# Gated delta rule in nine steps a tile instead of ten, with its norms in the next tile and part of the output projection beside its last steps

## The chip, the cores and the metric

One NeuronCore of one Trainium2 chip runs the whole program. The metric is the device time of one execution in microseconds (us); lower is better. The kernel before took 2258.96 us, the median of three runs (2255.09 to 2261.31).

## What is computed

Three residual blocks over 512 tokens of width 1024: two layers (mLSTM with forgetting attention; SSD with pooling), each with a convolved FFN, and then a third block, whose mixer is a gated delta rule (GDN) gated together with a sparse attention. The change touches only the GDN and the projection behind it. Cut to that:

```python
G = jnp.cumsum(gc, axis=-1)
gamma = jnp.exp(jnp.where(tri, G[..., :, None] - G[..., None, :], -jnp.inf))
A = jnp.where(strict, jnp.einsum("bnhid,bnhjd->bnhij", kb, kc) * gamma, 0.0)
T = lax.linalg.triangular_solve(A + eye, eye, left_side=True, lower=True)
v_new = u_i - jnp.einsum("bhcd,bhde->bhce", w_i, state)
o = jnp.einsum("bhcd,bhde->bhce", qg_i, state) + jnp.einsum("bhij,bhje->bhie", att_i, v_new)
state = state * dl_i[..., None, None] + jnp.einsum("bhcd,bhce->bhde", kd_i, v_new)
o_gdn = rmsnorm(o_gdn, gdn_norm_g[l]) * jax.nn.silu(z)
mixed = sigmoid(gate_a + gb[:D]) * o_gdn + sigmoid(gate_b + gb[D:]) * o_dsa
h = h + jnp.einsum("bse,ed->bsd", mixed, w_out[l])
```

## The kernel before

The weights are a stream of 333 units of 128x1024 fp32 that SP's queue loads into a ring of six slots. ACT rounds each unit to a high part (`whi`, L1015) and DVE subtracts it to get the low part (`wlo`, L1636); a product of two matrices is three matmuls, high by high, high by low, low by high (L370, L371, L372). A unit's slot is free when `units_done` counts it.

The GDN works on 4 tiles of 128 tokens and 8 heads. The heads are two groups `g` of four; group 0 owns PSUM banks 0 to 3, group 1 banks 4 to 7. A tile of a group goes through parts 0 to 9, written in each engine's program under `for c, g, part in gdn_order` (PE L909, ACT L1505, POOL L1596, DVE L2283). `gdn_order` sets every engine's order by hand: group 0 takes one part, then group 1 takes the part that lies five behind, and so on through 45 slots. The names in the code are these:

- part 0: `gb`, `bb`, `ge` (bf16 matmuls that spread gates and decays), `kq` (keys by queries); ACT makes `gam` and `eg`, DVE the gated keys `kb` (L2291), POOL copies the inverted 32x32 diagonal blocks into place (`placed`, L1605 and L1608);
- part 1: `kk`, then transposes `kt` and `vt` (L932, L938); DVE `at` (L2295) and `att` (L2298), POOL `kbg` and the squared queries `qq` (L1616);
- part 2: `x5`; DVE `kd` (L2301). Part 3: `y5`. Part 4: `x6`; DVE `qg` (L2314). Part 5: `y6`. These four products of 4 heads by 64 columns build the inverse of the 128x128 triangle from the small blocks, each waiting for a copy of the one before by ACT or DVE;
- part 6: `ks`, keys by state; DVE `r` (L2318). Part 7: `vn`, the new values; ACT copies them;
- part 8: `o`, the output (L984, L986), and `s`, the state's increment; ACT squares `o`, DVE adds the squared queries (L2322), gates `o` (`og`, L2323) and updates the state (L2328);
- part 9: `ms`, the mean of squares by a matmul with 1/128 (L997); ACT takes Ln and Exp (L1538, L1540), DVE scales (`scaled`, L2334), POOL adds into `MIX` (`mixed`, L1620).

The diagonal blocks are inverted before, by `substitute` on DVE (L2221, L2223), spread over the units of the projection `gatea` by the table `solved`, with two transposes after the last row (L2272, L2273).

After the last part ACT rounds `MIX` tile by tile (`split_tile`, L1038), DVE makes the low parts (L2343), and PE starts the projection `out2` with units 0 to 3 and tiles 0 to 2 (`token_products`, L444).

## Time and profile before

| | us |
|---|---|
| median of three runs | 2258.96 |
| the profiled execution | 2262.21 |
| its span | 2260.4 |
| busy: PE | 2196.7 |
| busy: DVE | 1297.4 |
| busy: ACT | 918.5 |
| busy: POOL | 110.7 |

The profile is of one execution. Busy time of PE is the time in which a matmul is in the array, counted to its modelled end, so back-to-back matmuls overlap: the distance from one start to the next is what a matmul costs. PEld is the load of its stationary operand. PEclk is the granted clock, 1.00 at 2.4 GHz and 0.50 at 1.2 GHz. "<-" names what ended an idle time. The GDN lies from 1711 us to 1834 us of the span.

### The profile page before, as it was taken

The page shows a single profiled execution, that of the slowest core. Times are in us where ns is not written, and L with a number is a line of the kernel's source. Part 1 is how long each engine was busy: PE and PEld are TensorE (multiplying, and loading weights), DVE is VectorE, ACT ScalarE, POOL GpSimd, SP SyncE. Part 2 cuts the span into 40 slices and gives each one's busy share as a digit, 9 for nine tenths or more (in the row PEclk, how much of TensorE's full clock was granted, in tenths as well). Part 3 has the DMA queues.
Part 4 walks back from the last instruction along what each step waited for, and adds up shares of the span by engine and source line. Part 5 has one row for each costly group of instructions (what it writes and reads, how often), then busy time and mean ns, then how long its engine had stood idle before and what let it go on. Part 6 is the DMA issues. An engine that isn't in the chain of part 4 may idle for free.

```text
span 2260.4 us, 26898 instructions
## 1 busy us (share of the span) xinstructions
PE 2196.7 (97%) x10736; PEld 1797.9 (80%) x10744; DVE 1297.4 (57%) x1995; ACT 918.5 (41%) x1544; POOL 110.7 (5%) x133
## 2 busy tenths in 40 slices
PE   8999999999999999999999999999998989999998
PEld 7867788888888668888888887776887868888887
DVE  6355475555347667555535439646786636555534
ACT  4135553334344545333434434344444434333431
POOL 1000040000000003000000000000002410000000
PEclk9999999999999999999999999999998999999999
DMA  5212223333323113333332222112221002333332
GB/s 198 89 56 75 66 85 94 102 94 111 103 71 105 58 45 105 94 101 95 111 104 77 88 88 75 47 44 78 84 85 38 1 32 81 95 101 94 117 98 75
DMA packets 50668, 189.82 MB, mean 84 GB/s; under 512 B 5617, under 2 KB 5617, under 8 KB 49777
## 3 DMA queue, kind: packets, MB, share of 16 engines
q1 hardware_dynamic: 50544, 188.11, 26.6%
q8 instruction: 86, 1.41, 0.3%
q14 instruction: 38, 0.30, 0.0%
HBM read 185.99 MB, written 2.10 MB: 83 GB/s over the span
## 4 chain that ended last, share of the span: by engine, by line
PE 89%; DVE 6%; ACT 2%; issue 2%; DMA 1%; ACTq 0%; DVEq 0%
PE bank L370 26%; PE bank L371 25%; PE bank L372 25%; PE bank L863 3%; PE bank L646 1%; PE bank L624 1%; PE bank L482 1%; PE bank L635 1%; PE bank L837 1%; DMA ring<-stream 1%; ACT whi L1015 1%; PE bank L562 1%; DVE small L1662 1%; DVE wlo L1636 0%; DVE small L1796 0%
## 5 line engine op out<-in xcount | busy, mean ns | idle before, releaser
L370 PE MATMUL bank<-xs,whi 128*128 128x512 f32 (+2 forms) x1992 | 772.8, 388 | 9.6 <-DVE xs L1984 7.8
L372 PE MATMUL bank<-xs,wlo 128*128 128x512 f32 (+2 forms) x1992 | 751.9, 377 | 0.0
L371 PE MATMUL bank<-xs,whi 128*128 128x512 f32 (+2 forms) x1992 | 751.4, 377 | 0.0
L1636 DVE TENSOR_TENSOR wlo<-ring,whi 128x1024 fp32r<-128x1024 f32 x333 | 415.1, 1249 | 317.4 <-ACT whi L1015 317.2
L1015 ACT ACTIVATE whi<-ring 128x1024 fp32r<-128x1024 f32 x333 | 350.1, 1053 | 283.1 <-DMA ring<-stream 280.8
L370 PEld LDWEIGHTS bank<-xs,whi 128*128 128x128 f32 x1992 | 376.9, 189 | 89.5 <-issue 7.9
L372 PEld LDWEIGHTS bank<-xs,wlo 128*128 128x128 f32 x1992 | 376.3, 189 | 69.5
L371 PEld LDWEIGHTS bank<-xs,whi 128*128 128x128 f32 x1992 | 377.2, 189 | 68.0 <-issue 3.3
L370 PE MATMUL bank<-whi,xs 128*128 128x512 f32 (+1 forms) x816 | 321.0, 393 | 9.8 <-DVE wlo L1636 5.7
L371 PE MATMUL bank<-wlo,xs 128*128 128x512 f32 (+1 forms) x816 | 317.9, 390 | 0.0
L372 PE MATMUL bank<-whi,xs 128*128 128x512 f32 (+1 forms) x816 | 317.5, 389 | 0.0
L1300 ACT ACTIVATE arena<-bank,par 128x512 f32<-128x512 f32 x132 | 103.0, 780 | 433.2 <-PE bank L372 433.2
L1927 DVE SCALAR_TENSOR_TENSOR arena<-bank,par,arena 128x511 f32<-128x511 f32 x132 | 98.9, 749 | 286.9 <-ACT arena L1300 286.7
L370 PEld LDWEIGHTS bank<-whi,xs 128*128 128x128 f32 x816 | 155.6, 191 | 43.0 <-DVE wlo L1636 7.5
L372 PEld LDWEIGHTS bank<-whi,xs 128*128 128x128 f32 x816 | 155.6, 191 | 31.9
L371 PEld LDWEIGHTS bank<-wlo,xs 128*128 128x128 f32 x816 | 155.8, 191 | 30.6 <-issue 0.2
L1929 DVE SCALAR_TENSOR_TENSOR arena<-bank,par,arena 128x510 f32<-128x510 f32 x132 | 98.8, 749 | 4.7
L1779 DVE SCALAR_TENSOR_TENSOR arena<-bank,par,arena 128x511 f32<-128x511 f32 (+2 forms) x96 | 71.8, 748 | 46.7 <-ACT arena L1461 36.2
L1571 POOL TENSOR_TENSOR arena<-arena 128x512 f32<-128x512 f32 x32 | 52.6, 1683 | 499.6 <-PE bank L482 307.1
L1152 ACT ACTIVATE arena<-bank,small 128x128 f32<-128x128 f32 (+3 forms) x64 | 33.7, 527 | 72.6 <-DVE small L1796 72.3
L1796 DVE TENSOR_REDUCE small<-bank 128x1 f32<-128x128 f32 (+3 forms) x64 | 31.2, 488 | 50.2 <-PE bank L626 46.8
L1461 ACT ACTIVATE arena<-bank,par 128x512 f32<-128x512 f32 x24 | 16.5, 687 | 87.6 <-PE bank L372 87.6
(319 smaller groups left out, 1927.9 us busy)
## 6 DMA issues: line engine op xcount, KB each, us to landing
ring<-stream SPq DMA_DIRECT2D x333, 512.0 KB, 3.6
arena<-gains SPq DMA_DIRECT2D x5, 1024.0 KB, 5.7
arena<-xt SPq DMA_DIRECT2D x4, 512.0 KB, 6.3
arena<-xn SPq DMA_DIRECT2D x1, 2048.0 KB, 7.9
out<-arena SPq DMA_DIRECT2D x4, 512.0 KB, 2.6
con<-consts SPq DMA_DIRECT2D x1, 744.0 KB, 11.6
arena<-brow SPq DMA_DIRECT2D x1, 512.0 KB, 12.3
par<-params SPq DMA_DIRECT2D x1, 407.5 KB, 8.0
```

The lines of the kernel that those rows point to most:

```text
L370: nc.tensor.matmul(out, ah, bh, start=first, stop=False)
L371: nc.tensor.matmul(out, ah, bl, start=False, stop=False)
L372: return nc.tensor.matmul(out, al, bh, start=False, stop=last)
L863: m = nc.tensor.matmul(tile(b)[:, hh, 0:n], l(hh), r(hh), start=start, stop=stop)
L1015: A(whi[:, v % SLOTS, :], ring[:, v % SLOTS, :], ACT.Copy).then_inc(whi_done, 1)
L1152: A(st["ps"][:, 0:W], bank[2 + n % 3][:, 0:W], ACT.Exp, bias=small[:, 200 + n % 4:201 + n % 4], accum_out=small[:, 204 + n % 4:205 + n % 4 ...
L1300: A(acc[:, s, :], bank_of(up, j)[:], ACT.Identity, bias=col(cols, 4 * j + 3), scale=col(cols, 4 * j + 2)).then_inc(scalar_out, scalar_at.n ...
L1571: nc.gpsimd.tensor_tensor(XT[:, tt, h], XT[:, tt, h], GB[:, i, h], op).then_inc(gpsimd_out, gpsimd_at.next("gained" if i == 0 else "shifte ...
L1636: V.tensor_tensor(wlo[:, v % SLOTS, :], ring[:, v % SLOTS, :], whi[:, v % SLOTS, :], ALU.subtract).then_inc(wlo_done, 1)
L1779: STT(dst[:, shift:], u[:, 0:SEQ - shift], w, dst[:, shift:], ALU.mult, ALU.add).then_inc(vector_out, vector_at.next())
L1927: STT(acc[:, s, 1:], u[:, 0:SEQ - 1], col(cols, 4 * j + 1), acc[:, s, 1:], ALU.mult, ALU.add).then_inc(vector_out, vector_at.next())
L1929: STT(acc[:, s, 2:], u[:, 0:SEQ - 2], col(cols, 4 * j), acc[:, s, 2:], ALU.mult, ALU.add).then_inc(vector_out, vector_at.next("conv", l, j))
```

## The change

- `LAG` is 4 and `STEPS` 9: group 1 lies four parts behind group 0, and part 9 is gone.
- The norm of a tile is done in the same group's next tile: sums of squares and `ms` in part 0, Ln and Exp in part 3, `scaled` in part 4, `mixed` on POOL in part 5. For that the outputs are kept in the place of the tile's queries (`outputs`), squares and roots in `kd`. The squared queries are made by ACT in part 6, no longer by POOL.
- `kq` moves from part 0 to part 3 and `att` to part 4; `kt` from part 1 to part 5 and `kd` to part 6, and both are left out in the last tile, which needs neither.
- The stationary operands of `x5` and `y5` have 96 columns, those of `x6` and `y6` 64, and the copies read the rows that are left.
- The splits of units 3, 4 and 5 of `out2`, three in a row in tile 1 before, are put into part 6 of three steps. The row table `solved` ends one unit of `gatea` earlier.
- In the last tile of group 1 the sixteen high-part products of tile 0 of `out2` (units 0 to 3) stand in parts 6 and 7; the eight low-part ones and the last `ms` follow the last part. `split_tile(0)` and `(1)` on ACT and the low part of tile 0 on DVE move up beside them.

```diff
-        HALF_STEP, STEPS = 5, 10
+        LAG, STEPS = 4, 9
+        out2_splits = {(0, 1): FIRST["out2"] + 3, (1, 0): FIRST["out2"] + 4, (1, 1): FIRST["out2"] + 5}
         gdn_order = []
-        for n in range(STEPS * TILES + HALF_STEP):
+        for n in range(STEPS * TILES + LAG):
             if n < STEPS * TILES:
                 gdn_order.append((n // STEPS, 0, n % STEPS))
-            if n >= HALF_STEP:
-                gdn_order.append(((n - HALF_STEP) // STEPS, 1, (n - HALF_STEP) % STEPS))
+            if n >= LAG:
+                gdn_order.append(((n - LAG) // STEPS, 1, (n - LAG) % STEPS))
...
+                    if (j, tt, half) in begun:
+                        done[j, tt, half] = nc.tensor.matmul(bank[b][:], xlo[:, slot(j), t], whi[:, s, w], start=False, stop=j == n - 1)
+                    else:
+                        done[j, tt, half] = products(bank[b][:], (xhi[:, slot(j), t], xlo[:, slot(j), t]), (whi[:, s, w], wlo[:, s, w]), j == 0, j == n - 1)
...
+                def high(j, tt, half):
...
+                    begun.add((j, tt, half))
+                    nc.tensor.matmul(bank[b][:], xhi[:, slot(j), t], whi[:, s, w], start=j == 0, stop=False)
+                    nc.tensor.matmul(bank[b][:], xhi[:, slot(j), t], wlo[:, s, w], start=False, stop=False)
...
                     if part == 0:
...
-                        claim(b + 3)
-                        pe.wait_ge(scalar_out, scalar_at.find("gqkv", 15))
-                        four(b + 3, lambda hh: gk[:, 4 * g + hh, cs], lambda hh: gq[:, 4 * g + hh, cs]).then_inc(tensor_out, tensor_at.next("kq", t))
...
+                        if c:
+                            mean_square(c - 1, g)
...
-                        four(b + 3, lambda hh: G["at"][:, hh, :], lambda hh: G["t5"][:, hh, :], n=64).then_inc(tensor_out, tensor_at.next("x5", t))
...
+                        four(b + 1, lambda hh: G["at"][:, hh, BLOCK:], lambda hh: G["t5"][:, hh, :], 3 * BLOCK, 64).then_inc(tensor_out, tensor_at.next("x5", t))
...
+                        four(b, lambda hh: G["at"][:, hh, 64:P], lambda hh: G["t6"][:, hh, :], 64, 64).then_inc(tensor_out, tensor_at.next("x6", t))
...
                     elif part == 6:
...
+                        if t == (TILES - 1, 1):
+                            mean_square(TILES - 1, 0)
+                            pe.wait_ge(scalar_out, scalar_at.find("xh", "mix2", 0))
+                            for j in (0, 1):
+                                for half in (0, 1):
+                                    out2_part.high(j, 0, half)
...
+                        reader[b + 1] = (SCALAR, ("sq", t)) if c < TILES - 1 else (VECTOR, ("og", t))
...
+                for j in range(4):
+                    for half in (0, 1):
+                        out2_part(j, 0, half)
+                mean_square(TILES - 1, 1)
...
+                    elif part == 3 and c:
+                        inverse_root(c - 1, g)
...
+                    elif part == 6:
+                        if t == (TILES - 1, 1):
...
+                        A(query_squares(c, g), outputs(c, g), ACT.Square).then_inc(scalar_out, scalar_at.next("qq", t))
+                        if t in out2_splits:
+                            split_units(out2_splits[t])
...
-                    nc.gpsimd.tensor_tensor(G["qq"], gq[:, 4 * g:4 * g + 4, cs], gq[:, 4 * g:4 * g + 4, cs], ALU.mult).then_inc(gpsimd_out, gpsimd_at.next("qq", t))
...
+                elif part == 5 and c:
+                    done = slice((c - 1) * P, c * P)
+                    pool.wait_ge(gpsimd_out, gpsimd_at.n)
+                    pool.wait_ge(vector_out, vector_at.find("scaled", (c - 1, g)))
+                    nc.gpsimd.tensor_tensor(MIX[:, 4 * g:4 * g + 4, done], MIX[:, 4 * g:4 * g + 4, done], outputs(c - 1, g), ALU.add).then_inc(gpsimd_out, gpsimd_at.next("mixed", (c - 1, g)))
...
-                solved = (8, 11, 14, 17, 20, 23, 26, 29, 31)
+                solved = (8, 12, 16, 19, 22, 25, 28, 31, 31)
...
                     if part == 0:
+                        if c:
+                            square_sums(c - 1, g)
                         dve.wait_ge(tensor_out, tensor_at.find("bb", t))
-                        if c:
-                            dve.wait_ge(vector_out, vector_at.find("scaled", (c - 1, g)))
                         V.tensor_tensor(G["kb"], gk[:, 4 * g:4 * g + 4, cs], tile(b + 1), ALU.mult).then_inc(vector_out, vector_at.next("kb", t))
...
                     elif part == 4:
+                        dve.wait_ge(tensor_out, tensor_at.find("kq", t))
+                        dve.wait_ge(vector_out, vector_at.find("at", t))
+                        V.tensor_tensor(G["gam"], tile(b + 2), G["gam"], ALU.mult).then_inc(vector_out, vector_at.next("att", t))
+                        if c:
+                            scaled(c - 1, g)
+                    elif part == 5:
+                        if t == (TILES - 1, 1):
+                            square_sums(TILES - 1, 0)
...
+                    elif part == 7:
+                        if t == (TILES - 1, 1):
+                            scaled(TILES - 1, 0)
+                            mixed(TILES - 1, 0)
                     elif part == 8:
-                        dve.wait_ge(scalar_out, scalar_at.find("sq", t))
-                        dve.wait_ge(gpsimd_out, gpsimd_at.find("qq", t))
-                        STT(G["gam"], G["qq"], RMS_EPS * P * P, G["gam"], ALU.mult, ALU.add).then_inc(vector_out, vector_at.next("sq", t))
-                        STT(gated, tile(b + 1), small[:, 224:225], z2[:, 4 * g:4 * g + 4, cs], ALU.mult, ALU.mult).then_inc(vector_out, vector_at.next("og", t))
+                        if t == (TILES - 1, 1):
+                            dve.wait_ge(tensor_out, tensor_at.find("vn", t))
+                            tile_low(0)
+                        dve.wait_ge(tensor_out, tensor_at.find("o", t))
+                        dve.wait_ge(scalar_out, scalar_at.find("qq", t) if c < TILES - 1 else scalar_at.find("sq", t))
+                        dve.wait_ge(vector_out, vector_at.find("qg", t))
+                        STT(outputs(c, g), tile(b + 1), small[:, 224:225], z2[:, 4 * g:4 * g + 4, cs], ALU.mult, ALU.mult).then_inc(vector_out, vector_at.next("og", t))
...
+                square_sums(TILES - 1, 1)
+                tile_low(1)
+                tile_low(2)
+                scaled(TILES - 1, 1)
+                mixed(TILES - 1, 1)
+                tile_low(3)
```

How the orders move, at three places. In the names, bank0 to bank3 are group 0 and bank4 to bank7 group 1.

PE, around the end of part 8 of group 0 in a middle tile. Before (L863 is `s`, then `y5` of group 1, L997 `ms`, L863 `x6`, then part 0 of group 1):

```order
L863 MATMUL bank6<-arena,scratch 128x128 x4
L863 MATMUL bank0<-scratch 128x64 x4
L997 MATMUL bank7<-arena,inv128 128x512
L863 MATMUL bank2<-scratch 128x64 x4
L868 MATMUL bank4<-arena 128x128
...
L863 MATMUL bank5<-arena 128x128 x4
```

and now (L892 `s`, `x6` of group 1, the gates of group 0's next tile, L942 its `ms`, L892 `y6`, L1001 `kt`):

```order
L892 MATMUL bank2<-arena,scratch 128x128 x4
L892 MATMUL bank4<-scratch 64x64 x4
L897 MATMUL bank0<-arena 128x128
L898 MATMUL bank0<-mtb,idb 128x128
...
L892 MATMUL bank1<-arena 128x128 x4
L892 MATMUL bank2<-arena 128x128 x4
L942 MATMUL bank3<-scratch,inv128 128x512
L892 MATMUL bank5<-scratch 64x64 x4
L1001 MATMUL bank6<-con,arena 128x128 x4
```

`ms` of a tile now stands behind the gates of the next tile, and `y6`, `kt` and the next `kk` stand behind it.

DVE, behind part 8 of one group. Before (sums of squares L2322, `og` L2323, the state L2328, `decays` and `qg` of the other group L2310 and L2314, `scaled` L2334, the next `kb` L2291):

```order
L2322 SCALAR_TENSOR_TENSOR arena<-scratch,arena 128x512
L2323 SCALAR_TENSOR_TENSOR scratch<-bank,small,arena 128x512
L2328 SCALAR_TENSOR_TENSOR arena<-arena,small,bank 128x128 x4
L2310 COPY small<-arena 128x4
L2314 TENSOR_TENSOR arena<-arena 128x512
L2334 TENSOR_TENSOR scratch<-scratch,arena 128x512
L2291 TENSOR_TENSOR arena<-arena,bank 128x512
L2318 TENSOR_TENSOR scratch<-scratch,bank 128x512
```

and now (`og` L2430, the state L2435, `att` and `scaled` of the other group L2395 and L2360, the sums of squares L2354, the next `kb` L2381):

```order
L2430 SCALAR_TENSOR_TENSOR arena<-bank,small,arena 128x4x128
L2435 SCALAR_TENSOR_TENSOR arena<-arena,small,bank 128x128 x4
L2395 TENSOR_TENSOR arena<-bank,arena 128x512
L2360 TENSOR_TENSOR arena<-arena,scratch 128x4x128
L2354 SCALAR_TENSOR_TENSOR scratch<-scratch 128x512
L2381 TENSOR_TENSOR arena<-arena,bank 128x512
L2402 COPY small<-arena 128x4
L2406 TENSOR_TENSOR arena<-arena 128x512
L2385 SCALAR_TENSOR_TENSOR scratch<-bank,arena 128x512
```

The sums of squares, for which `ms` waits, left the place ahead of `og` and stand behind the state and two operations of the other group.

PE at the end. Before (L863 is `x6`, `y6`, `ks`, `vn` of group 1, L984 and L986 `o`, L997 `ms`, then `out2`):

```order
L863 MATMUL bank7<-arena,scratch 128x128 x4
L863 MATMUL bank4<-scratch 128x128 x4
L984 MATMUL bank5<-arena 128x128
L986 MATMUL bank5<-arena 128x128
...
L997 MATMUL bank7<-arena,inv128 128x512
L370 MATMUL bank0<-whi,xs 128x512
L371 MATMUL bank0<-wlo,xs 128x512
L372 MATMUL bank0<-whi,xs 128x512
```

and now (L892 is `x6`, `y6`, `ks`, L942 the `ms` of group 0, L467 and L468 high-part products, L892 `vn`, L1036 and L1038 `o`, L453 low-part products):

```order
L892 MATMUL bank4<-scratch 64x64 x4
L892 MATMUL bank5<-scratch 64x64 x4
L892 MATMUL bank7<-arena,scratch 128x128 x4
L942 MATMUL bank3<-arena,inv128 128x512
L467 MATMUL bank0<-whi,xs 128x512
L468 MATMUL bank0<-wlo,xs 128x512
...
L892 MATMUL bank4<-scratch 128x128 x4
L467 MATMUL bank0<-whi,xs 128x512
...
L1036 MATMUL bank5<-arena 128x128
L1038 MATMUL bank5<-arena 128x128
...
L453 MATMUL bank1<-whi,xs 128x512
...
L942 MATMUL bank7<-arena,inv128 128x512
L383 MATMUL bank2<-whi,xs 128x512
```

Twenty-four products of `out2` that stood behind the last `ms` now lie around `vn` and `o`.

## Rows read from the trace of the kernel before

**Rows 1.** The page: busy time and share of each engine over the span.

```profile
PE 2196.7 (97%) x10736; PEld 1797.9 (80%) x10744; DVE 1297.4 (57%) x1995; ACT 918.5 (41%) x1544; POOL 110.7 (5%) x133
```

**Rows 2.** Windows: stretch, its length, busy time (instructions) per engine, PEclk, DMA.

```profile
1711.13:1739.04 27.91, 23.07 (x164) 21.23 (x164) 14.15 (x26) 12.77 (x32) 9.69 (x22) 0.82 0.06 20
1739.04:1769.59 30.55, 25.93 (x215) 24.03 (x215) 20.19 (x37) 15.74 (x37) 12.00 (x22) 0.94 0.00 1
1769.59:1796.71 27.12, 25.89 (x230) 24.27 (x230) 17.34 (x35) 12.79 (x34) 11.99 (x22) 1.00 0.01 2
1796.71:1817.40 20.69, 20.33 (x188) 19.51 (x188) 13.71 (x25) 10.33 (x29) 10.70 (x21) 1.00 0.00 1
1817.40:1845.51 28.11, 19.33 (x103) 15.49 (x102) 12.39 (x18) 10.98 (x17) 1.29 (x2) 0.88 0.00 1
```

**Rows 3.** Timeline of PE, second to third tile: start, us, line, operation, count.

```profile
1759.32 1.06 PE L863 MATMUL bank<-arena 128*128 128x128 f32 x8
1760.21 0.60 PE L932 MATMUL bank<-con,arena 128*128 128x128 f32 x4
...
1763.16 0.44 PE L984 MATMUL bank<-arena 128*128 128x128 f32 x2
...
1765.00 1.06 PE L863 MATMUL bank<-arena,scratch 128*128 128x128 f32 x8
1765.90 1.00 PE L863 MATMUL bank<-scratch 128*128 128x64 f32 x8
1766.74 1.08 PE L997 MATMUL bank<-arena,inv 128*128 128x512 f32 x2
...
1771.45 1.00 PE L863 MATMUL bank<-scratch 128*128 128x64 f32 x8
```

**Rows 4.** Groups by form: weight loads of 128 and of 8 columns.

```profile
L863 PEld LDWEIGHTS bank<-scratch 128*128 128x128 f32 x320 | 40.6, 199 | 13.2 <-DVE scratch L2305 6.0 <-ACT scratch L1524 2.9 <-DVE arena L2298 2.0
...
L601 PEld LDWEIGHTS bank<-arena,con 128*8 128x8 f32 x16 | 0.8, 87 | 2.8 <-issue 2.8
```

**Rows 5.** Timeline of DVE, third tile.

```profile
1770.13 1.71 DVE L2314 TENSOR_TENSOR arena<-arena 128x512 f32<-128x512 f32 x1
...
1782.41 1.11 DVE L2328 SCALAR_TENSOR_TENSOR arena<-arena,small,bank 128x128 f32<-128x128 f32 x4
...
1783.71 0.69 DVE L2314 TENSOR_TENSOR arena<-arena 128x512 f32<-128x512 f32 x1
```

**Rows 6.** Timeline of POOL, same stretch.

```profile
1770.02 1.26 POOL L1620 TENSOR_TENSOR arena<-arena,scratch 128x512 f32<-128x512 f32 x1 [5.57 <-DVE small L2310]
```

**Rows 7.** Timeline of DVE, end of the projection before the delta rule.

```profile
1709.74 0.21 DVE L2221 TENSOR_TENSOR arena<-arena 128x60 f32<-128x60 f32 x1
...
1710.69 2.02 DVE L2272 STREAM_TRANSPOSE arena<-arena 128x1024 f32<-128x1024 f32 x1
```

**Rows 8.** Timeline of all engines, last steps of the last tile.

```profile
1824.81 1.11 PE L863 MATMUL bank<-arena,scratch 128*128 128x128 f32 x8
...
1825.96 0.69 DVE L2318 TENSOR_TENSOR scratch<-scratch,bank 128x512 f32<-128x512 f32 x1 [0.23 <-PE bank L863]
...
1826.79 1.13 PE L863 MATMUL bank<-scratch 128*128 128x128 f32 x8 [0.87 <-DVE scratch L2318]
```

**Rows 9.** Timeline of PE, start of the output projection.

```profile
1837.35 0.77 PE L370 MATMUL bank<-whi,xs 128*128 128x512 f32 x1 [4.07 <-issue]
...
1845.51 0.39 PE L370 MATMUL bank<-whi,xs 128*128 128x512 f32 x1
```

**Rows 10.** Windows of a few microseconds, for PEclk.

```profile
1716.00:1720.00 4.00, 4.00 (x22) 3.73 (x22) 1.98 (x3) 1.88 (x7) 3.45 (x10) 0.58 0.00 0
1724.00:1730.00 6.00, 5.49 (x34) 5.47 (x34) 0.90 (x2) 2.38 (x7) 0.00 (x0) 0.50 0.01 3
1750.50:1754.00 3.50, 3.50 (x18) 3.50 (x18) 2.81 (x6) 0.60 (x1) 0.00 (x0) 0.53 0.00 0
1828.00:1836.00 8.00, 3.12 (x18) 2.16 (x18) 2.63 (x4) 4.75 (x7) 0.00 (x0) 1.00 0.00 0
```

190 lines of the change are left out of this document (110 added, 80 removed).

## Prediction

> **What bounds the kernel now.** PE is busy for 97% of the span [rows 1], so elsewhere only PE's own work counts. I read the delta rule apart, by windows from one `gb` of group 0 to the next: the first two tiles take 27.9 and 30.6 us, a settled one 27.1, the last one 20.7 to group 0's `o`, and from there it is 28.1 to the point at which 24 of `out2`'s products are issued [rows 2]. Together 134.4 us, the only stretch that the change touches. In the settled tile PE is the limit: it is busy for 25.9 of the 27.1 [rows 2] and its starts follow each other [rows 3]. In the two first tiles and at the end it waits for the other engines, and the clock falls with it [rows 2, 10].
>
> **PE's work in half a tile.** From start to start, four fp32 products of 128 columns cost 0.90 us, eight (`o`) 1.84, four of 64 columns 0.84 [rows 3]. The time shown for a group is 0.16 longer than that, for its modelled end; so four transposes are 0.44 and `ms` 0.91. From `gb` at 1769.59 to `y6` at 1771.45 lie the bf16 gates and `kq` [rows 2, 3]: 1.86, less 0.90, leaves 0.95 for the gates. Before, each group's tile holds `o`, five of 0.90, two sets of transposes, four of 0.84, `ms` and the gates: 12.4 us, so 24.9 for both groups, and 27.1 with waits.
>
> **The narrower operands.** The 64-column products cost as much as a load of 128 columns, 0.105 us each, half of what their moving side alone would need being below it (128 columns take 0.11). A load took 199 ns for 128 columns and 87 ns for 8 [rows 4], so about 0.9 ns a column. With 96 columns each of the eight takes 0.08 and the four 0.64; with 64, 0.053 and 0.43. That is 2 x 0.20 + 2 x 0.41 = 1.2 us less per half tile (one group's tile): 11.2. The bounds are 0 (a load is no shorter for fewer columns) and 1.2; I take 1.2, since the two rows differ so widely.
>
> **What takes the place of it.** The new order puts `ms` of a tile behind a queue on DVE. From the issue of the last `s` product: 0.25 to its result, the state 1.14, `att` 0.61, `scaled` 0.61, the sums of squares 0.69, 0.14 to PE: 3.4 us (durations [rows 5, 8], each 0.08 less where the next one follows, whose start overlaps; the lags, 0.04 to DVE and 0.14 to PE, [rows 8]). Meanwhile PE has only `x6` 0.43 and the gates 0.95, so it waits 2.0 us, and `y6`, `kt` and the next `kk` stand behind `ms`. Two smaller waits, for `x5`'s copies and for `r`, add 0.8. Half a tile is then 11.2 + 2.8 = 14.0, a tile 27.8: in a settled tile the change gives back more than the narrower operands win.
>
> **The walk.** To get the four stretches I walked every engine's queue through both orders, each instruction at the later of its engine's free time and its releaser's end plus the lag, with the durations above. Of the order before it gives 30.5, 26.8 and 20.5 us for tile 1, tile 2 and the way from the last `gb` to the last `o` of group 0, where the trace has 30.6, 27.1 and 20.7. Of the new order:
> - Tile 0: 19.0 at full clock. The trace has 27.9 where the walk has 23.8 at full clock and 28.2 with the clock halved in the first two stretches of [rows 10]. The rows of `substitute` that no longer stand in the last unit of `gatea` are 0.95 us of DVE [rows 7] on the way to the first `kb`. The first wait of PE stays over 2 us, so the clock falls once or twice again: 20.3 or 22.5. I take 22.0, 5.9 less than before.
> - Tile 1: 27.2, 3.4 less. The three splits in a row, behind which PE waited, are spread.
> - Tile 2: 27.8, 0.7 more.
> - The end: 39.8, 9.0 less. Up to `o` of group 0 it is 23.6 against 20.7, two more waits for `ms`. From there, before, 28.1 us: six waits of PE, 8.8 in all, 0.87 ahead of `vn` [rows 8] and 4.07 ahead of the first product; and 24 products in 8.2 us, where at 0.23 each (0.39 less 0.16) they take 5.5: 2.7 for the clock [rows 9]. Now PE has `o` 1.8, `x6` and `y6` 0.9, `ks` 0.9, `ms` 0.9, high parts 1.8, `vn` 0.9, high parts 1.8, `o` 1.8, low parts 1.8, `ms` 0.9: 13.5, and waits 0.8 for `x6`'s copy, 1.0 for the sums of squares and 0.8 at the last `ms`: 16.1. No wait is long, so I leave the clock at full. The tile's own transposes `kt`, left out here, are 0.9 of it.
>
> Sum: 22.0 + 27.2 + 27.8 + 39.8 = 116.8 against 134.4. I take 17 of the 17.6, since the walk of the order before came out 0.6 short over 78 us. The profiled execution took 2262.2, so 2245.2; it stood 3.3 above the median of 2258.96, so the median becomes **2242.0**.
>
> **Taken at nothing.** ACT gets the squared queries, 0.6 us twice a tile, from POOL: it is busy 12.8 of 27.1 us [rows 2] and they lie behind `ks`, where it has nothing to do. If that cover were gone, `vn`'s copy would be late by 0.6. POOL loses 1.04 us per half tile. No DMA moves: the ring's slots are freed by `units_done` as before, and SP's queue issues the same loads. The first six `gatea` units carry up to one more row pair of `substitute` on DVE, whose splits are three units ahead.
>
> **A rule against a row.** `qg` on DVE took 1.71 us while POOL's L1620 ran from 0.11 us before it, and 0.69 alone [rows 5, 6]: it waited until POOL was done. In the walk such waits cost 0.9 us in all. The Trainium skill ("SBUF — State Buffer", "Who interferes with whom") says more: a DVE instruction with two SBUF inputs and a GpSimd instruction that reads SBUF exclude each other for a whole instruction, whoever comes first. By it `scaled` and the sums are stopped as well where they meet POOL. POOL is busy for 12.0 of 27.1 us with 22 instructions [rows 2], 0.55 us each; three such instructions in each of eight half tiles, met 44 times in 100 and halfway, would wait 24 x 0.44 x 0.27 = 2.9 us, 2 more than in the sum; that is inside the range.
>
> **The rivals.**
> 1. *The clock falls in each half tile.* PE's wait for `ms` is 1.7 to 2.0 us, with small gates beside it. Behind longer waits of PE in the first two tiles the clock was at half for 3.5 to 6 us; against it, from 1828 to 1836 PE was busy 3.1 of 8 us and the clock stayed 1.00 [rows 10]. If each of the six middle waits is followed by 3.4 us at half, the walk gives 126.2 for the 116.8: 8.2 gained, **2251**. The Trainium skill ("TensorE: Matmul & The Clock Gate", "What's actually happening") calls the throttled clock the default that only activity releases, which speaks for this one. Chance 0.15.
> 2. *Narrow operands load no faster.* The walk is then 5.1 longer: 2242 + 5 = **2247**. Against it, the 87 ns row. Chance 0.07.
> 3. *The clock stays down through the delta rule.* Half a tile is then 11.2 x 2 + 2 = 24.4 instead of 14, six times: 62 more, **2304**. It decides from about 34 us at 1.2 GHz, where 17 us of PE's work doubled eat the gain. Before, it was down for some 20 us of 134, and PE's share of work now falls from 92% to 80% of the time. Chance 0.04.
> 4. *The high parts do not fill.* They stand in PE's queue ahead of `vn` and wait for ACT's rounding of tile 0, which waits for POOL's last sums. In the walk it is 1.2 us early; late by 3, the end is 3 longer: **2245**. Chance 0.06.
>
> **How the numbers follow.** The forecast has 0.68, its own range 2236 to 2249: tile 0 between 20.3 and 24, and 3 us either way for the medians, whose runs spread over 6. Rivals 1, 2 and 4 are faster too, 1 hardly. Range for 8 in 10: 2235 to 2253. A difference under 0.3%, 6.8 us, is not told from none: faster means below 2252.2. That is 0.68 + 0.08 + 0.06 + 0.04 = 0.86; same 0.09, slower 0.05.
>
> **What would show it.** The profile after should show, counted from the first `gb`: the second some 22 us later, then 27 and 28; PE's `ms` preceded by an idle time of 1.5 to 2 us put down to DVE's sums of squares; the four products of 64 columns start to start in 0.43 and those of 96 in 0.64; PEclk 1.00 from tile 1 to the end; and no gap over 1.1 us between group 0's last `o` and the first product of tile 1 of `out2`, 16 us apart. I am wrong if a settled tile is under 26 or over 29 us, or if the end is not 8 us shorter.

## The result and the profile after

| | before | after |
|---|---|---|
| median, us | 2259.75 | 2243.45 |
| lowest to highest | 2255.09 to 2261.31 | 2242.39 to 2246.15 |
| profiled execution | 2262.21 | 2243.9 |
| its span | 2260.4 | 2242.1 |

Four runs of each; the ratio is 0.9929, 95% interval 0.9916 to 0.9943, 16 us less. Forecast were 2242.0 and faster. The page:

```profile
PE 2180.8 (97%) x10728; PEld 1779.5 (79%) x10736; DVE 1300.5 (58%) x1993; ACT 923.6 (41%) x1552; POOL 106.2 (5%) x125
```

The stretches between the `gb` of group 0, then to its last `o` and to the first product of tile 1 of `out2` (windows, columns as in [rows 2]):

```profile
1708.95:1731.45 22.50, 18.39 (x157) 16.41 (x156) 10.90 (x21) 11.81 (x31) 9.64 (x28) 0.85 0.09 24
1731.45:1758.65 27.20, 23.07 (x214) 20.11 (x213) 18.07 (x34) 15.87 (x39) 10.87 (x19) 1.00 0.01 2
1758.65:1788.68 30.03, 26.14 (x230) 23.10 (x228) 20.15 (x36) 14.92 (x38) 11.01 (x20) 0.94 0.01 1
1788.68:1812.70 24.02, 20.62 (x194) 18.27 (x193) 16.82 (x31) 13.08 (x36) 7.98 (x12) 1.00 0.00 1
1812.70:1828.81 16.11, 14.63 (x95) 11.60 (x93) 10.28 (x15) 7.68 (x12) 1.58 (x1) 1.00 0.00 1
```

119.86 us where [rows 2] have 134.38, 14.5 less. The two spans differ by 18.3. The rest lies outside: the first `gb` stands at 1708.95 instead of 1711.13, and from the last point to the end it is 413.3 us instead of 414.9. Whether the 2.2 us ahead of the stretch are scatter is not settled. In the twelve other profiles of this study, whose code up to there is nearly the same, the first `gb` lies between 1705.96 and 1711.19. But the two profiles of the order before have the two latest, 1711.13 and 1711.19, and they alone show the clock at 0.50 for 3.4 us at 1440 us; the twelve of the changed order end at 1710.44. The 1.6 us behind it are about one more stretch at half clock, which the profile before has at 1867 us.

A settled half tile (PE's timeline, from one `gb` at 1788.68 to the next at 1802.58; the gates' bf16 products stand between the first two rows):

```profile
1788.07 0.68 PE L892 MATMUL bank<-scratch 128*64 128x64 f32 x8
...
1789.16 0.61 PE L892 MATMUL bank<-arena 72*128 72x128 bf16 x8
1791.25 1.10 PE L942 MATMUL bank<-scratch,inv 128*128 128x512 f32 x2 [1.48 <-DVE scratch L2354]
1792.28 0.68 PE L892 MATMUL bank<-scratch 128*64 128x64 f32 x8
1792.88 0.66 PE L1001 MATMUL bank<-con,arena 128*128 128x128 f32 x4
...
1796.63 1.78 PE L892 MATMUL bank<-scratch 128*128 128x128 f32 x16 [0.22 <-ACT scratch L1595]
```

The reader is to see one wait, 1.48 us ahead of `ms` (L942), put down to DVE's sums of squares (L2354), and one of 0.22 ahead of `vn`. The row names ACT's squares (L1595) for the second; by the program PE waits there for `r`, which DVE ended 0.14 us earlier, and never for the squares. And from start to start: `y6`, four products with 64 columns loaded, take 0.60 (1792.28 to 1792.88), not 0.43. DVE in the same moments:

```profile
1788.18 1.12 DVE L2435 SCALAR_TENSOR_TENSOR arena<-arena,small,bank 128x128 f32<-128x128 f32 x4
1789.22 0.68 DVE L2395 TENSOR_TENSOR arena<-bank,arena 128x512 f32<-128x512 f32 x1
1789.82 0.68 DVE L2360 TENSOR_TENSOR arena<-arena,scratch 128x512 f32<-128x512 f32 x1
1790.42 0.68 DVE L2354 SCALAR_TENSOR_TENSOR scratch<-scratch 128x512 f32<-128x512 f32 x1
1791.02 0.68 DVE L2381 TENSOR_TENSOR arena<-arena,bank 128x512 f32<-128x512 f32 x1
...
1792.36 1.76 DVE L2406 TENSOR_TENSOR arena<-arena 128x512 f32<-128x512 f32 x1
```

State, `att`, `scaled`, sums of squares, `kb`: PE's `ms` stands behind the fourth. The weight loads (groups by form, tiles 1 to 3; beside [rows 4]):

```profile
L892 PEld LDWEIGHTS bank<-arena,scratch 128*128 128x128 f32 x80 | 9.7, 192 | 0.0
L892 PEld LDWEIGHTS bank<-scratch 128*96 128x96 f32 x88 | 8.5, 165 | 2.6 <-ACT scratch L1577 2.6
...
L892 PEld LDWEIGHTS bank<-scratch 128*64 128x64 f32 x80 | 5.8, 146 | 4.7 <-issue 4.1
```

Half tile 20 to 21 (`gb` of group 0 of tile 2 to that of group 1) took 16.14 us instead of 13.9. The clock fell behind its wait for `ms`:

```profile
1762.00:1764.00 2.00, 2.00 (x11) 1.33 (x11) 1.90 (x2) 0.30 (x1) 1.47 (x2) 0.50 0.00 0
1764.00:1766.00 2.00, 2.00 (x15) 2.00 (x14) 0.11 (x2) 0.08 (x1) 0.00 (x0) 0.68 0.00 0
```

The clock is 1.6 of the 2.2 us, and 0.7 is a split. From `ms` to `y5` it is 8.54 us here and 6.99 in the half tile before it, which has the same split and full clock. In both, ACT's split of a unit stands ahead of `x5`'s copies, and PE waits for them (ACT, PE); in the settled half tile above, without a split, it does not:

```profile
1767.95 1.07 ACT L1066 ACTIVATE whi<-ring 128x1024 fp32r<-128x1024 f32 x1
```

```profile
1769.76 0.86 PE L892 MATMUL bank<-scratch 128*96 128x64 f32 x8 [0.48 <-ACT scratch L1577]
```

And the end, where [rows 8] and [rows 9] show waits of 0.87 and 4.07 us (PE; `y6`, `ms` of group 0, `ms` of group 1, tile 1 of `out2`; the high and low parts of tile 0 stand between the two `ms`):

```profile
1815.79 0.65 PE L892 MATMUL bank<-scratch 128*64 128x64 f32 x8 [0.53 <-ACT scratch L1582]
...
1818.08 1.10 PE L942 MATMUL bank<-arena,inv 128*128 128x512 f32 x2 [0.55 <-DVE arena L2354]
...
1827.76 1.10 PE L942 MATMUL bank<-arena,inv 128*128 128x512 f32 x2 [0.40 <-DVE arena L2354]
1828.81 0.50 PE L383 MATMUL bank<-whi,xs 128*128 128x512 f32 x1
```

No wait over 0.55 is left, and from `o` at 1812.70 to 1828.81 it is 16.1.

### The profile page after: what moved, and what is told of

It reads as the page before. It is cut to its first block, busy times and chain, and to the rows that moved or that the text cites. A ratio compares the mean times of both kernels' runs of the same rounds, so it can differ in the third digit from the quotient of the medians.

```text
span 2242.1 us, 26904 instructions
## 1 busy us (share of the span) xinstructions
PE 2180.8 (97%) x10728; PEld 1779.5 (79%) x10736; DVE 1300.5 (58%) x1993; ACT 923.6 (41%) x1552; POOL 106.2 (5%) x125
## 4 chain that ended last, share of the span: by engine, by line
PE 88%; DVE 7%; ACT 3%; issue 2%; DMA 1%; POOL 0%; DVEq 0%; ACTq 0%; POOLq 0%
PE bank L383 26%; PE bank L385 25%; PE bank L384 25%; PE bank L892 2%; PE bank L675 1%; PE bank L653 1%; DMA ring<-stream 1%; ACT whi L1066 1%; PE bank L511 1%; DVE small L1729 1%; PE bank L664 1%; PE bank L866 1%; PE bank L591 1%; DVE arena L1756 1%; DVE wlo L1703 0%
## 5 line engine op out<-in xcount | busy, mean ns | idle before, releaser
L383 PE MATMUL bank<-whi,xs 128*128 128x512 f32 (+1 forms) x808 | 315.5, 391 | 5.6 <-DVE wlo L1703 5.6
L384 PE MATMUL bank<-wlo,xs 128*128 128x512 f32 (+1 forms) x808 | 312.6, 387 | 0.0
L385 PE MATMUL bank<-whi,xs 128*128 128x512 f32 (+1 forms) x808 | 312.5, 387 | 0.0
L383 PEld LDWEIGHTS bank<-whi,xs 128*128 128x128 f32 x808 | 152.8, 189 | 37.8 <-DVE wlo L1703 7.4
L385 PEld LDWEIGHTS bank<-whi,xs 128*128 128x128 f32 x808 | 152.8, 189 | 31.0
```

The lines of the kernel that those rows point to most:

```text
L383: nc.tensor.matmul(out, ah, bh, start=first, stop=False)
L384: nc.tensor.matmul(out, ah, bl, start=False, stop=False)
L385: return nc.tensor.matmul(out, al, bh, start=False, stop=last)
```

## Experiments

All are edits of the changed kernel but for one of the kernel before. They were measured in four groups on different chips, each beside the kernel before, whose medians were 2258.5 to 2259.6 us; medians of different groups compare to about 1 us. Half tiles are read from `gb` to `gb`; "a drop" is a stretch in which one-microsecond windows show the granted clock at 0.50.

### The changed kernel again

This run is called the repeat below.

> The changed kernel once more, word for word, beside the runs of one change to it each. Theory of a noisy clock: half tile 20 to 21 took 16.1 us in the first profile because the granted clock was 0.69 from 1760 to 1765; in this profile the half tiles from the second gb of tile 1 on are all 13.9 (within 0.2), and the drop stands elsewhere or is not there, so that the stretch from the first gb to the first product of tile 1 of out2 is 117.5 rather than 119.9 us. Rival, a drop that the program causes: the same half tile is 16 us again. The part ahead of the first gb, whose code is the same but for the rows of substitute, ended 2.2 us earlier than before: if that is scatter between executions, this profile puts it anywhere between 1708.5 and 1711.5. Time against the kernel before: 0.993, as in the first measurement.

Measured: 2244.2 us (2242.92 to 2246.06, 5 runs), ratio to before 0.9939 (0.9927 to 0.9950). Windows of its profile, tile 2 and the end, from the last `gb` of group 0 to the first product of tile 1:

```profile
1757.41:1787.46 30.05, 26.17 (x231) 22.74 (x229) 20.16 (x36) 14.92 (x38) 11.02 (x20) 0.94 0.01 1
1787.46:1829.15 41.69, 36.81 (x287) 31.09 (x285) 27.15 (x45) 20.74 (x47) 9.56 (x13) 0.96 0.00 1
```

The half tile 20 to 21 is 16.14 again, to the hundredth: the rival holds there, the drop comes from the program. But a second drop, at 1804, was not in the first profile and costs 1.6 (26.23 from the last `gb` to tile 1 became 27.79), and tile 0, with the clock at half for 3.4 us instead of 6.8, was 1.1 shorter (21.39). Where a drop falls is partly the program's, partly not. The first `gb` came at 1708.82 once more.

### 128 columns loaded again

```
-four(b + 1, lambda hh: G["at"][:, hh, BLOCK:], lambda hh: G["t5"][:, hh, :], 3 * BLOCK, 64)
+four(b + 1, lambda hh: G["at"][:, hh, :], lambda hh: G["t5"][:, hh, :], P, 64)
...
```

The same for `y5`, `x6`, `y6`; the copies read the rows where the results then stand.

> The changed kernel with the four small product groups (x5, y5, x6, y6) loading 128 columns again, and nothing else changed. Theory (a load costs its columns, 0.9 ns each, and the loads set the pace of a 64-column product): each group is 0.84 us from start to start instead of 0.64 and 0.43, a half tile 1.2 longer in PE's work; the walk through the queues gives 5.1 us more than the changed kernel (some of it falls into waits): 2248.5 against 2243.4, the settled tile 29.0 instead of 27.8. Rival, the products are paced by something other than the number of columns loaded: 0 us, and 0.84 in both. Second rival, PE's work does not matter since DVE's queue ahead of ms sets the half tile: under 1.5 us, with the idle time ahead of ms shorter by what the products are longer.

Measured: 2248.4 us, 12 runs from 2241.5 to 2258.0, far more scattered than the others; ratio to before 0.9960 (0.9946 to 0.9974). The profiled run was the slowest:

```profile
1710.44:1739.89 29.45, 25.83 (x157) 24.54 (x157) 11.06 (x22) 12.07 (x31) 9.64 (x28) 0.65 0.05 19
1739.89:1767.69 27.80, 24.33 (x215) 22.44 (x214) 18.11 (x35) 15.85 (x39) 10.54 (x19) 1.00 0.01 1
1767.69:1798.41 30.72, 27.48 (x231) 25.30 (x231) 20.18 (x36) 14.90 (x38) 10.99 (x20) 0.94 0.01 1
1798.41:1840.63 42.22, 38.50 (x287) 33.61 (x286) 27.04 (x44) 20.59 (x47) 9.55 (x13) 0.96 0.00 1
```

In its tile 0 the clock stood at 0.50 for 20 us, from 1716 to 1736, though PE had work for 25.8 of 29.5 us. Where the clock is full, the half tiles are 13.15, 14.65 and 14.18 us where the changed kernel has 12.85, 14.35 and 13.90: 0.3 longer each, not 0.6 as in the walk; the wait ahead of `ms` shrank from 1.48 to 1.35. So the second rival is right about the settled tiles: the work saved falls mostly into waits for DVE. The windows at full clock give 2 to 2.5 us in all; the median's 4.2 are nearer to the walk's 5.1, but where the rest lies no run shows. The scatter goes with the clock: the mean granted clock of the twelve runs goes from 0.995 (2241.5 us) to 0.986 (2258.0 us), four of them at 0.988 or less, and the two fastest are under every run of the changed kernel. At 0.992 and 0.993 the wide runs took 2246.1 to 2247.2 us, the changed kernel's 2242.4 to 2246.2.

### The narrow operands alone, in the kernel before

```
-four(b, lambda hh: G["at"][:, hh, :], lambda hh: G["t6"][:, hh, :], n=64)
+four(b, lambda hh: G["at"][:, hh, 64:P], lambda hh: G["t6"][:, hh, :], rows=64, n=64)
...
```

> The kernel before with the narrower operands alone: x5, y5, x6 and y6 load 96, 96, 64 and 64 columns and write as many rows, ten steps a tile and all else as before. Theory: the walk through the order before gives 2.4 us less, 2257.3 for 2259.7 (of 1.2 us a half tile, 9.6 in all, three quarters fall into waits of PE behind DVE and ACT). Rival, PE's work is the whole limit in this stretch: 8 to 10 us less, 2250.5. Rival, the load is no shorter for fewer columns: 0.

Measured: 2254.7 us, 3.8 less than before (0.9986, 0.9978 to 0.9995). Its third tile took 26.85 us, before 27.12 [rows 2]: nearly nothing at full clock. 2.9 of the gain in its profile lie in tile 0 (24.98 instead of 27.91), where the clock was at half for 6.8 us instead of 10.2. In the third tile PE was busy for 24.67 us instead of 25.89, and its waits grew by nearly as much. So the prediction's reading that PE is the limit in a settled tile does not hold: what is taken off PE's work there comes back as waits. The rival of 8 to 10 us falls. The rival of 0 falls by the shorter loads, shown above, but its time at full clock is near; the walk's 2.4 came close to 3.8, much of which went through the clock.

### No high parts beside the last steps

```
-if t == (TILES - 1, 1):
-    for j in (2, 3):
-        for half in (0, 1):
-            out2_part.high(j, 0, half)
...
```

The same four lines for units 0 and 1, and the wait ahead of them, go out of part 6; all 24 products then stand behind the last `o`.

> The changed kernel without the high-part products beside the last steps: the sixteen products of units 0 to 3 and tile 0 of out2 that stood ahead of and behind vn stand with their low parts behind the last o, where nothing waits for them. The number of products is the same. Theory: the high parts fill waits of the last half tile (for y6, r and vn); the walk gives the first product of tile 1 of out2 4.1 us later, 2247.5. If the clock falls in the waits that open, it is up to 3 more. Rival, the high parts delay vn and o by as much as they fill: under 1.5 us.

Measured: 2247.2 us, 3.0 more than the repeated kernel (0.9950, 0.9938 to 0.9962). PE's waits behind `ms` of group 0, for `vn` and for `o`, are there again:

```profile
1819.48 1.10 PE L942 MATMUL bank<-arena,inv 128*128 128x512 f32 x2 [0.56 <-DVE arena L2346]
1822.02 1.13 PE L892 MATMUL bank<-scratch 128*128 128x128 f32 x8 [1.45 <-ACT arena L1553]
1823.88 0.46 PE L1028 MATMUL bank<-arena 128*128 128x128 f32 x2 [0.73 <-ACT arena L1592]
```

1.45 and 0.73 us, which the changed kernel fills. From the last `gb` to the first product that waits for a new unit of `out2`'s weights it is 48.27 us against 46.25 in the repeat, with one drop in both: 2.0. The two intervals overlap a little, so of the median's 3.0 the profile's 2.0 are the surer part. I had expected 4.1 from a walk that put the 24 products behind the last `ms`; they stand ahead of it and cover its wait. Corrected in that, the walk gives 1.7.

### The splits together, and the old table of rows

```
-out2_splits = {(0, 1): FIRST["out2"] + 3, (1, 0): FIRST["out2"] + 4, (1, 1): FIRST["out2"] + 5}
+out2_splits = {(1, 0): FIRST["out2"] + SLOTS - 1}
```

(issued in part 2), and in another kernel

```
-solved = (8, 12, 16, 19, 22, 25, 28, 31, 31)
+solved = (8, 11, 14, 17, 20, 23, 26, 29, 31)
```

> The changed kernel with the splits of units 3, 4 and 5 of out2 together on ACT and DVE in part 2 of tile 1 of group 0, as the kernel before had them, instead of one each in part 6 of three half tiles. Theory: PE waits some 3 us in that half tile behind DVE's three splits in a row, and less in the half tiles that are freed of one; the walk gives 1.3 us more in all, 2245.3; with a clock drop behind that wait, as the kernel before shows one there, 2 to 3 us more, 2247.5. Rival, the spread brings the whole gain of tile 1, 3.4 us: 2247.4 without a drop of the clock.

> The changed kernel with the old table of rows for the last units of gatea: two rows of the substitution on DVE stand in its last unit again. Theory: these 0.95 us of DVE are on the way to the first kb, so PE's first wait is 3.4 instead of 2.5 us and the time 0.9 more, 2244.9; and if the clock falls for longer behind it, up to 3 more. Rival, the 2.2 us by which the changed kernel's first gb came earlier (1708.95 against 1711.13) come from this table and not from scatter: the first gb is at 1711 again and the time 2 to 3 us more.

Measured: 2244.18 us with the splits together (0.9936, 0.9923 to 0.9949), so no difference to the repeat's 2244.2. Tile 1 took 29.81 instead of 27.20, with a drop in it, and tile 2 27.80 instead of 30.05, without one. The drop has only moved. With 1.6 us taken off for each drop, tile 1 is 1.0 longer and tile 2, which has no split left in it, 0.7 shorter: the spread is worth some 0.4 us, an estimate, where the walk had 1.3. With the old table 2245.1 us (0.9935, 0.9923 to 0.9947), 0.9 more, PE's first wait 3.38 instead of 2.53, as the theory had both, though the scatter of the runs (2241 to 2249) is larger than the effect. The first `gb` was at 1706.89, so the rival falls: the table is not what moved it.

### `ms` later in PE's order; `kb` first on DVE

Two moves that add no work. On PE `mean_square(c - 1, g)` from the end of part 0 to part 2, behind `x5`:

```
                         reader[b + 2] = (SCALAR, ("eg", t))
-                        if c:
-                            mean_square(c - 1, g)
...
                         reader[b + 1] = (SCALAR, ("x5", t))
+                        if c:
+                            mean_square(c - 1, g)
```

and, in another kernel, on DVE `square_sums(c - 1, g)` from ahead of `kb` to behind it.

> The changed kernel with the product ms of the tile before moved in PE's order alone: from behind the gates of part 0 to behind x5 in part 2. No other engine's order changes, no work is added. Theory (PE waits 1.48 us in each settled half tile because DVE still has state, att, scaled and the sums of squares ahead of it, and y6, kt and kk stand behind ms): with ms later these products run in the wait, the idle time ahead of ms goes to under 0.3, the walk gives 24.3 and 25.9 us for tiles 1 and 2 instead of 27.2 and 27.8, and 5.8 us in all: 2238 for the changed kernel's 2244. If the drops of the clock in the half tile 20 to 21 come from that wait, they go too, 2 to 4 us more: 2235. Rival, the half tile is set by DVE and ACT and not by this wait: PE waits as long elsewhere (for kb, at or kd), under 1 us gained.

> The changed kernel with two DVE instructions swapped: kb of the tile ahead of the sums of squares of the tile before, PE's order as it is. Theory (ms is what PE waits for, and whatever stands ahead of the sums on DVE lengthens that wait): the idle time ahead of ms grows from 1.48 by about kb's 0.6, in six half tiles, 3.6 us in all, 2247.6; with the clock falling more often behind the longer wait up to 4 more. Rival, the wait for kb behind ms is what counts: 0 or a gain of up to 3.

Measured: **2240.6 us** with `ms` later (0.9914, 0.9901 to 0.9927), 3.6 less than the repeat, and **2258.8 us** with `kb` first (0.9999, 0.9991 to 1.0008), 14.5 more: swapping two DVE instructions of 0.6 us gives back the whole gain. With `ms` later no wait ahead of the six middle `ms` is left, and from the second `gb` to tile 1 the clock is 1.00. But the settled half tile is 13.63, not 13.0: of the wait of 1.48 only 0.27 us come back. PE now waits for `kb` and `at`:

```profile
1772.99 1.13 PE L892 MATMUL bank<-arena 128*128 128x128 f32 x8 [0.89 <-DVE arena L2381]
...
1775.96 0.86 PE L892 MATMUL bank<-scratch 128*96 128x64 f32 x8 [0.52 <-DVE scratch L2385]
```

`at` comes late since DVE's copy of the decays and `qg`, ahead of it, meet two sums on POOL (DVE and POOL):

```profile
1772.76 0.64 DVE L2402 COPY small<-arena 128x4 f32<-128x4 f32 x1
1773.50 1.76 DVE L2406 TENSOR_TENSOR arena<-arena 128x512 f32<-128x512 f32 x1
1775.19 0.68 DVE L2385 SCALAR_TENSOR_TENSOR scratch<-bank,arena 128x512 f32<-128x512 f32 x1
```

```profile
1771.79 1.58 POOL L1687 TENSOR_TENSOR arena<-arena 128x512 f32<-128x512 f32 x1 [3.96 <-DVE arena L2360]
1773.44 1.27 POOL L1682 TENSOR_TENSOR scratch<-arena 128x512 f32<-128x512 f32 x1
```

0.64 for a copy that takes 0.16 alone, and 1.76 for `qg` instead of 0.69. With `kb` first the sums of squares themselves are caught (DVE, POOL, PE):

```profile
1782.23 0.68 DVE L2379 TENSOR_TENSOR arena<-arena,bank 128x512 f32<-128x512 f32 x1
1782.83 1.44 DVE L2354 SCALAR_TENSOR_TENSOR scratch<-scratch 128x512 f32<-128x512 f32 x1
```

```profile
1782.46 1.26 POOL L1687 TENSOR_TENSOR arena<-arena 128x512 f32<-128x512 f32 x1 [3.91 <-DVE arena L2360]
```

```profile
1784.41 1.56 PE L942 MATMUL bank<-scratch,inv 128*128 128x512 f32 x2 [2.84 <-DVE scratch L2354]
```

The sums start 0.37 us after POOL's sum and last 1.44 instead of 0.68, so `ms` waits 2.84: 1.48, 0.60 for `kb`, 0.76 for POOL. The clock then fell five times from tile 1 on, once for twice as long (the sixth fall that the expectation below counts lies in tile 0). From the first `gb` to tile 1 of `out2` it is 133.6 us against 120.3 in the repeat: by the rows some 7 of the 13.3 are longer waits in six half tiles, and some 6 are four more stretches at half clock, at 1.6 each. `kb`, one of whose operands is in PSUM, ran beside POOL's sum in its 0.68.

### POOL's sum behind `kbg`; `qg` behind `kd`

```
-                elif part == 5 and c:
+                elif part == 6 and c:
                     done = slice((c - 1) * P, c * P)
```

on POOL, once in the kernel with `ms` later and once in the one with `kb` first; and a kernel with `ms` later, `kb` first, and DVE's copy of the decays and `qg` moved from part 5 to part 6, behind `kd`.

> The kernel with ms later (2240.6) and one more move: POOL's sum of the tile before into MIX in part 6 instead of part 5, so behind kbg of the other group instead of ahead of it. In the profile with ms later, DVE's copy of the decays took 0.64 beside that sum and qg 1.76 beside kbg, and the product x5 waited 0.52 us for at, which stands behind both on DVE. Theory (a DVE instruction with both operands in SBUF waits for a POOL instruction that is under way, and this is on the path to x5): the copy is back at 0.16, qg ends 0.5 earlier, PE's wait for x5 goes, and the settled half tile is 13.0 us instead of 13.6; the walk gives 5.0 us less in all, about 2236. Rival, the sum then collides with something else that matters (r, kd or the decays of the next half tile): within 1 us of 2240.6.

> The kernel with kb ahead of the sums of squares (2258.8, 14.5 more than the changed kernel where 3.6 was expected), and POOL's sum into MIX in part 6 instead of part 5. In its profile the sums of squares took 1.44 us instead of 0.68, beginning while POOL's sum was under way, and ms waited 2.84 us for them instead of 1.48; the clock fell six times. Theory (0.6 of the longer wait is kb, 0.76 is DVE held by POOL, the rest of the 14.5 is the clock behind the longer waits): with the sum moved the sums take 0.68 again, ms waits 2.1, the half tile is 0.8 us shorter at full clock, 4 us in all, 2254.5; if fewer drops of the clock follow, 1.7 less for each. Rival, the 0.76 is not POOL's: nothing changes.

> The kernel with ms later (2240.6), and on DVE kb ahead of the sums of squares, and the copy of the decays and qg behind kd in part 6 instead of in part 5. In the profile with ms later PE still waited 0.89 us for kb and 0.52 for at in each settled half tile, while DVE stood idle for 2.3 and 1.8 us later in it. Theory (what PE waits for in a half tile is the order of DVE's queue, not DVE's work): both waits go, the half tile falls from 13.6 to 12.3 us, and the walk gives 8.6 us less in all, 2232; with no wait over 1 us in the middle tiles the granted clock is 1.00 there. Rival, o waits for the later qg instead: half tile 13 or more, 2236 or more.

Measured: **2235.8** (0.9897, 0.9884 to 0.9911), **2253.7** (0.9973, 0.9964 to 0.9983) and **2232.2** (0.9881, 0.9867 to 0.9894), where 2236, 2254.5 and 2232 were expected. In the second the sums of squares took 0.69 again and `ms` waited 2.08:

```profile
1779.42 0.68 DVE L2379 TENSOR_TENSOR arena<-arena,bank 128x512 f32<-128x512 f32 x1
1780.02 0.69 DVE L2354 SCALAR_TENSOR_TENSOR scratch<-scratch 128x512 f32<-128x512 f32 x1
```

That settles the 0.76 as POOL's. In the third the settled half tile is 12.29 us, with one wait of 0.28 in it, and the clock is full from the second `gb` on (windows; PE's timeline, DVE's):

```profile
1756.38:1781.21 24.83, 24.24 (x231) 21.99 (x229) 18.40 (x36) 14.64 (x38) 10.91 (x20) 1.00 0.01 2
```

```profile
1771.47 1.13 PE L892 MATMUL bank<-arena 128*128 128x128 f32 x8 [0.28 <-DVE arena L2379]
```

```profile
1771.24 1.45 DVE L2354 SCALAR_TENSOR_TENSOR scratch<-scratch 128x512 f32<-128x512 f32 x1
...
1775.18 0.16 DVE L2412 COPY small<-arena 128x4 f32<-128x4 f32 x1
1775.44 0.69 DVE L2416 TENSOR_TENSOR arena<-arena 128x512 f32<-128x512 f32 x1
```

The sums of squares are caught by POOL here too (1.45), but PE reaches `ms` only later and does not wait; `qg` behind `kd` meets no one. This version beats both kernels: 26.5 us under the one before, 12 under the changed one.

### The first wait filled

The kernel is the last one above (2232.2), with ten products whose results nobody reads in PE's first wait:

```
                     elif part == 1:
+                        if t == (0, 0):
+                            claim(b + 3)
+                            pe.wait_ge(scalar_out, scalar_at.find("gqkv", 15))
+                            for i in range(10):
+                                nc.tensor.matmul(tile(b + 3)[:, i % 4, :], gk[:, i % 4, cs], gq[:, i % 4, cs], start=True, stop=True)
```

> The fastest kernel so far (ms later, kb first, qg later; 2232.2) with ten products of 128 columns more, whose results nobody reads, in PE's first wait of the stretch, the 2.53 us for the first kb. Nothing else is changed; by 0.225 us each they take 2.25 of the 2.53. Theory (the drop of the clock some 1 us behind that wait, 3.4 or 6.8 us at half, comes from the wait): PE waits 0.3 us, the granted clock stays 1.00 from the first to the second gb, and the way between them is 19.0 us, as in the walk at full clock, instead of 22.5: 3.4 us less, 2228.8, though the kernel does more work. Rival, the waits behind it (0.25 for POOL's copies, 0.74 for x5's copies) or the part ahead are enough for the drop: the same 21.4 or 22.5 us and 2232, or up to 0.3 more for the added products.

Measured: **2230.4 us**, four runs within 1.1 us (0.9874, 0.9858 to 0.9891). One of the four runs without the ten products was faster still, 2229.6.

```profile
1708.88 2.45 PE L964 MATMUL bank<-arena 128*128 128x128 f32 x20
1711.58 1.13 PE L892 MATMUL bank<-arena 128*128 128x128 f32 x8 [0.24 <-DVE arena L2384]
```

```profile
1707.71:1728.01 20.30, 18.09 (x177) 16.34 (x176) 10.90 (x21) 11.79 (x31) 9.64 (x28) 1.00 0.09 27
```

The first wait is 0.24 and the clock 1.00 from the first `gb` to the second, 20.30 us apart instead of 22.55: with nothing but these products added, the drop is gone, so the first wait made it, and the later waits of 0.43 and 0.74 alone do not. All thirteen other profiles show a drop there. 2.25 us of the stretch came back, 1.8 of them in the median. One drop appeared elsewhere, at 1834 in the output projection. The walk had 19.0 us for this stretch at full clock; it is 20.30, though `kk` starts as long behind `gb` as without the products (3.87 us).

## Why the prediction was right, point by point

| step | before | forecast | after | repeat |
|---|---|---|---|---|
| tile 0 | 27.91 | 22.0 | 22.50 | 21.39 |
| tile 1 | 30.55 | 27.2 | 27.20 | 27.20 |
| tile 2 | 27.12 | 27.8 | 30.03 | 30.05 |
| the end | 48.80 | 39.8 | 40.13 | 41.69 |
| sum | 134.38 | 116.8 | 119.86 | 120.33 |
| execution, us | 2262.21 | 2245.2 | 2243.9 | 2244.2 |

- **The time** was met in part by luck. The stretch gave back 14.5 us (14.1 in the repeat) where the sum has 17.6; 2.2 us ahead of it and 1.6 behind it, which no step had foreseen, went the other way.
- **The prediction's own signs of being wrong** came up. It named a settled tile over 29 us, and tile 2 took 30.03 and 30.05; it named an end not 8 us shorter, and in the repeat the end is 7.1 shorter (8.7 in the first profile).
- **The walk of the queues** was right in tile 1, and at full clock without a split the half tiles are 13.9 against 14.0, but through errors that cancel, below. The sum came out 3.1 short: in tile 2, 1.6 for the drop and 0.7 for the split on ACT; 0.5 in tile 0 and 0.3 at the end.
- **"Tile 0: 19.0 at full clock"** was 1.3 too short: with the first wait filled it is 20.30 with the clock at 1.00. With 3.4 us at half the tile takes 21.39, with 6.8 us 22.50. The 22.0 was met since the walk was too short and the clock cheaper (1.1 for each 3.4 us at half, where the walk had 1.3 for the first and 2.2 for the second).
- **"With 64, 0.053 and 0.43"** failed. The narrower operands load in 165 and 146 ns against 192, and a group of 64 columns takes 0.60 from start to start (96 columns: 0.65, as forecast). The loads lie near the line through the 87 ns of 8 columns and the 199 of 128, which gives 169 and 139. What failed is the step from the load to the pace, 0.105 us taken down in proportion to the columns: at 64 the pace is 0.075, not 0.053, and what holds it there no run shows. PE saves 0.86 us a half tile, not 1.2.
- **"It waits 2.0 us" for `ms`** was right in place and cause, and too large: 1.48 shown, 1.6 from start to start. Counted from start to start, PE's work in the half tile was 11.9 instead of 11.2 (half of it the 64 columns, the rest some 0.1 each in `ms`, `kt`, `s` and `y5`), and its waits 2.0 instead of 2.8: they cancelled. The sums later on DVE lost 14.5 us. `ms` later on PE gained 3.6, but only 0.27 in the settled half tile, since PE then waits for `kb` and `at`. What sets the half tile is thus the order of DVE's queue as a whole: with three moves in it and in PE's it is 12.29.
- **The clock.** "PEclk 1.00 from tile 1 to the end" failed. Rival 1 (a drop in each half tile) is right in kind and in price, but holds in one or two of six. A drop costs 1.6 us in tile 2 and at the end; the rival's walk has 9.4 for six, 1.6 each.
- **The end** was 8.7 us shorter (forecast 9.0), in the repeat with its drop 7.1. From `o` on 16.1 was forecast and 16.11 measured, again by errors that cancel: waits of 0.53, 0.55 and 0.40 instead of 0.8, 1.0 and 0.8, and PE busy for 14.63 us instead of 13.5. The high parts are 2 of it by the profile and 3.0 in the median, so rival 4 is out; they were in time, and the wait of 4.07 ahead of `out2` is gone.
- **The three splits**: 3.4 us less in tile 1 is right, but spreading them is not what brings it to the whole: together they cost nothing that the median shows, and where each of them lands, in tile 2 too, it delays `x5`'s copies.
- **The rows of `substitute`**: 0.95 forecast; PE's first wait is 0.85 longer with the old table.
- **DVE and POOL.** 0.9 us was in the walk, 2 more in the range. In the changed order `scaled` and the sums run in 0.68, just ahead of POOL; in the settled half tiles only the copy and `qg` are caught, and with nothing of PE's waiting. The Trainium skill ("SBUF — State Buffer", "Who interferes with whom") says that the order of issue decides which of the two engines is blocked. The rows of the two orders agree: the sums take 0.68 ahead of POOL's sum, which then takes 1.58, and 1.44 behind it, where POOL's takes 1.26.
- **ACT's squares at nothing** ("where it has nothing to do") failed in part. `x5`'s copies stand right behind them. In a settled half tile the copies end 0.4 us before PE needs them; in the three half tiles in which a split stands there too, PE waited 1.17, 0.48 and 0.48 us. A square takes 0.65; a kernel without them was not run.

By the medians, without the narrow operands it is 4.2 more, without the high parts 3.0, with the old rows 0.9, with the splits together 0. About 7 of the 15 us are left for the order itself and for what the clock does in it; no run takes these apart. By PEclk in the windows the clock was at half for some 20 us of the stretch before and for some 10 after; at the 1.1 to 1.6 us that 3.4 us at half cost here, that is 3 to 5 us, an estimate.

## What to carry to other kernels

Walk every engine's queue with measured durations: three kernels were forecast within 1 us of their medians in that way, and a wait of 1.5 us turned up that PE's 97% hid. The walk does not give the clock, nor a meeting of DVE and POOL that the new order makes: `kb` first was forecast at 2247.6 and took 2258.8. Look at the terms too, since a right sum can hide two wrong ones. When an engine waits for the last of several instructions on another, first move the waiting product behind work that is ready, before cutting anything. Then look for the next wait, which took most of that gain here. And place a DVE instruction with both operands in SBUF where POOL is idle or only just about to start, or where nobody waits for it.
